# Two mixers of a two-block transformer on one core: x taken ahead of the high parts in a written-out first mixer, the second mixer's first projections in the first one's block, and output products in the second mixer's last head

## The chip, the cores and the metric

The kernel runs on one core of a Trainium2 chip. The metric is the device time of one execution in microseconds (us). A measured time is the median of several runs; the trace comes from one further, profiled execution.

## The reference, cut to what matters

Four layers over 1024 tokens of width 1024, all in float32. The change touches only the first of them:

```python
def rglru_hgrn2_layer(u, w_in, w_out, ...):
    proj = jnp.einsum("bsd,de->bse", u, w_in)
    rg_x, rg_g, hg_q, hg_f, hg_i, hg_g = jnp.split(proj, ...)
    h = rglru_mixer(rg_x, conv_w, conv_b, w_a, b_a, w_x, b_x, lam)
    o = hgrn2_mixer(hg_q, hg_f, hg_i, lb)
    o = o * lax.rsqrt(jnp.mean(o * o, axis=-1, keepdims=True) + RMS_EPS) * g_norm
    merged = jnp.concatenate([h * jax.nn.silu(rg_g), o.reshape(...) * jax.nn.silu(hg_g)], axis=-1)
    return merged @ w_out
```

The first mixer (`rglru_mixer`) takes the x branch through a causal convolution of 4 taps, makes two sigmoid gates of it by 64-wide block matrices, forms `a = exp(log_a)` and `b = sqrt(1 - a*a) * (gate_i * xc)`, and runs the linear recurrence `h = a*h + b` over the tokens. The second (`hgrn2_mixer`) is gated linear attention with 8 heads of width 128, in chunks, with a decay per channel. `merged` has 2048 columns and is multiplied by a 2048 x 1024 matrix. An RWKV-7 layer and two hybrid attention layers follow.

## The kernel before

The program is a row of blocks; a block has one instruction stream per engine, and all engines meet at its end before the next begins. TensorE (PE) does the matmuls, ScalarE (ACT) and VectorE (DVE) everything elementwise, GpSimd (POOL) splits the very first weights, SyncE (SP) issues the DMAs.

Each float32 product is done in float16 in three matmuls: a value is split into a high part and a low part (`w_hi`, `w_lo`; `u_hi`, `u_lo`; `m_hi`, `m_lo`), and high x high, high x low, low x high are summed in PSUM. A projection (`channel_major`, L131; `token_major`, L147) is 8 blocks of the inner dimension x 2 halves x 3 = 48 matmuls of 128x512, or 192 of 128x128. Weights come in units of 512 KB through a ring of 4 slots: SP loads `stage` (`load_unit`), ACT makes the high part (`split_high`, L109), DVE the low part (`split_low`, L115). `K.w_full[slot]` counts units split, `K.w_free[slot]` units used; SP may load a slot when its unit before has been split, ACT may split when PE has used it. Sources are taken one round ahead.

**First mixer** (`rglru`). Four rounds in a hardware loop (`Fori`), each for two tiles of 128 channels. PE's order in a round: x of tile 0, gate branch of tile 0, x of tile 1, gates of tile 0, gate branch of tile 1, gates of tile 1. The x branch uses PSUM banks 0 and 1, the gate branch 2 and 3. Before an x projection PE waits for `x_taken`, which DVE raises (L476) once ACT has copied the x before to `xb` (L425); the first is raised at the end of DVE's setup (L467), a softplus of `lam`. DVE does the convolution (L477 to L482), the product of the gate branch (L486), then the low parts of the next weights. After both tiles ACT does tanh, exp, square and square root, DVE the scan, and its product goes to `m_hi` (ACT, L450) and `m_lo` (DVE, L508). ACT takes the next round's x at the head of that round, so behind both `m_hi` copies.

**Second mixer** (`hgrn2`). PE projects f, q, g and v of head 0 first. Its start waits for `g_taken`, which DVE raises (L798) behind its setup: memsets, and the lower bounds `lb` and `oml` from a softmax (to L795), for which ACT does one exp (L757). `take_f` on ACT (two sigmoids, L679 and L680) needs f and `raw_free`, also raised there, and comes in ACT's order behind `lb_ready`. g may be projected when f is taken, v when q is. In the steady state a head's five level batches of small float32 matmuls (L603), the transposition of k (L613), the state steps (L621), the output (L629, L630) and the norm (L637) stand between the projections of the next head. The last head has no next one, so only those stand there. Its norm comes after it, alone.

**Output projection** (`project_out`, tag out0). First half (output columns 0 to 511): for each of 8 units of `w_out`, for each of 8 token tiles t, 6 matmuls into bank t (L1063). Units 0 to 3 are in the ring slots at the start, split during head 6. Second half: for each t, all 8 units from a held copy. SP's order is low-rank weights, gain, held units 0 to 3, x (8 loads of 512 KB, L1019), ring units 4 to 7, held units 4 to 7. ACT and DVE split in that order.

## Time and profile before

| | |
|---|---|
| three runs | 3682.11, 3686.03, 3684.61 us; median 3684.61 |
| the profiled execution | 3681.23 us, span 3679.2 us |
| PE busy | 3348.3 us, 91% of the span |
| DVE, ACT, POOL busy | 1877.1, 1406.7, 551.2 us |
| TensorE clock granted, mean | 0.961 of 2.4 GHz |
| start-up, to the first mixer's block | 0 to 46.7 us |
| first mixer | to 293 us |
| second mixer | to 839 us |
| output projection out0 | 840.5 to about 1013 us |

Times within a view are microseconds from the span's start. A row of a timeline is start, duration, engine, line, operation, output and inputs; in brackets stands how long the engine had been idle and who released it. "DVEq" or "PEq" is a semaphore instruction of that engine's queue. A busy PE of 100% does not mean full speed: matmuls overlap, so what counts is the time from the start of one to the start of the next.

### The profile page before, as it was taken

How to read it: one execution, taken by the hardware profiler on the slowest of the kernel's cores; microseconds unless marked ns; L12 is line 12 of the kernel's file. 1: busy time of each engine (PE TensorE's matmuls, PEld its weight loads, DVE VectorE, ACT ScalarE, POOL GpSimd, SP SyncE). 2: the span in 40 equal slices, each digit the busy share in tenths (PEclk: the TensorE clock that was granted, in tenths of full speed). 3: DMA queues.
4: the chain of work that ended last, by engine and by line, in shares of the span. 5: the costliest groups of instructions: out<-in, count | busy, mean ns of one | idle time of the engine just before them, and what ended most of it. 6: DMA issues, size and time to landing. Idle time of an engine off the chain costs nothing. (4 is left out here: it accounts for less than half of the span.)

```text
span 3679.2 us, 72862 instructions
## 1 busy us (share of the span) xinstructions
PE 3348.3 (91%) x32106; PEld 2085.2 (57%) x32106; DVE 1877.1 (51%) x2548; ACT 1406.7 (38%) x2026; POOL 551.2 (15%) x350
## 2 busy tenths in 40 slices
PE   6987999978979898999998899989889999899889
PEld 3334666663434343999996466647434566657334
DVE  4654566662253833666663566644352366633442
ACT  3553444442354632333332445533211355523211
POOL 3000000002000001333331133200150232100330
PEclk9998999979989999999999999999999999999999
DMA  5101110104035643111113111020120211020211
GB/s 166 34 23 50 30 40 29 40 0 149 1 107 118 153 115 114 64 64 64 63 45 105 52 46 40 2 62 24 39 82 27 66 38 35 1 68 18 62 62 46
DMA packets 308329, 215.24 MB, mean 59 GB/s; under 512 B 125411, under 2 KB 283950, under 8 KB 305454
## 3 DMA queue, kind: packets, MB, share of 16 engines
q1 hardware_dynamic: 307608, 210.70, 19.2%
q8 instruction: 230, 3.77, 0.4%
q10 hardware_dynamic: 442, 0.37, 0.0%
q14 instruction: 49, 0.40, 0.0%
HBM read 173.26 MB, written 41.98 MB: 59 GB/s over the span
## 5 line engine op out<-in xcount | busy, mean ns | idle before, releaser
L142 PE MATMUL psum<-u,w_hi 128*128 128x512 f16 x2816 | 855.8, 386 | 103.1 <-DVEq L798 32.0
L142 PE MATMUL psum<-u,w_lo 128*128 128x512 f16 x1408 | 542.4, 385 | 0.0
L142 PEld LDWEIGHTS psum<-u,w_hi 128*128 128x128 f16 x2816 | 279.1, 100 | 452.4 <-issue 55.6
L97 POOL TENSOR_TENSOR w_hi<-stage,w_scale 128x1024 f16<-128x1024 f32 x52 | 99.4, 1912 | 1244.8 <-PE psum L142 600.0
L1063 PE MATMUL psum<-w_hi,merged 128*128 128x512 f16 x768 | 236.1, 389 | 24.9 <-PEq L2887 9.1
L115 DVE SCALAR_TENSOR_TENSOR w_lo<-stage,w_hi 128x1024 f16<-128x1024 f32 x124 | 149.3, 1220 | 186.1 <-ACT w_hi L109 186.0
L2475 DVE CUSTOM_DVE_ANT_0 probs_att<-psum,bias_att 128x1024 f32<-128x1024 f32 x128 | 156.8, 1225 | 167.8 <-PE psum L2287 167.6
L142 PEld LDWEIGHTS psum<-u,w_lo 128*128 128x128 f16 x1408 | 139.8, 99 | 172.8 <-issue 11.9
L2265 PE MATMUL psum<-u,w_hi 128*128 128x512 f16 x768 | 231.6, 383 | 6.3 <-PEq L966 6.3
L1063 PE MATMUL psum<-held_hi_out,merged 128*128 128x512 f16 x768 | 231.0, 379 | 0.0
L157 PE MATMUL psum<-w_hi,u 128*128 128x128 f16 x2048 | 173.2, 219 | 0.0
L157 PE MATMUL psum<-w_lo,u 128*128 128x128 f16 x1024 | 172.3, 219 | 0.0
L142 PE MATMUL psum<-mix_b_rp,w_hi 128*128 128x512 f16 x512 | 153.6, 382 | 11.9 <-DVE mix_b_rp L1569 11.4
L157 PEld LDWEIGHTS psum<-w_hi,u 128*128 128x128 f16 x2048 | 158.0, 98 | 4.9 <-issue 4.6
L2384 ACT ACTIVATE probs_att<-probs_att,neg_max_att 128x1024 f32<-128x1024 f32 x128 | 146.3, 1146 | 19.5 <-DVE neg_max_att L2479 19.4
L2315 PE MATMUL psum<-turned_att,merged 128*128 128x128 f32 x1024 | 139.7, 281 | 15.0 <-ACT sq_att L2398 14.6
L2099 DVE COPY_PREDICATED Tt_rc<-tmask_rc,psum 128x256 f32<-128x256 uint32 x192 | 83.6, 444 | 131.9 <-PE psum L1789 110.9
L1063 PE MATMUL psum<-w_lo,merged 128*128 128x512 f16 x384 | 149.4, 389 | 0.0
L2315 PEld LDWEIGHTS psum<-turned_att,merged 128*128 128x128 f32 x1024 | 132.2, 195 | 27.7 <-issue 17.7
L109 ACT ACTIVATE w_hi<-stage 128x1024 f16<-128x1024 f32 x124 | 127.6, 1048 | 53.2 <-PE psum L1063 42.3
L1063 PEld LDWEIGHTS psum<-w_hi,merged 128*128 128x128 f16 x768 | 76.6, 100 | 124.4 <-issue 38.3
L2265 PE MATMUL psum<-u,w_lo 128*128 128x512 f16 x384 | 146.9, 382 | 0.0
(444 smaller groups left out, 6804.8 us busy)
## 6 DMA issues: line engine op xcount, KB each, us to landing
stage<-w_in SPq DMA_DIRECT2D x72, 512.0 KB, 4.0
X<-rwkv_chunks SPq DMA_DIRECT2D x14, 1792.0 KB, 8.0
stage<-ab_w_in SPq DMA_DIRECT2D x48, 512.0 KB, 4.9
stage<-rw_w_in SPq DMA_DIRECT2D x32, 512.0 KB, 4.7
rwkv_chunks<-work_rp SPq DMA_DIRECT2D x26, 512.0 KB, 6.0
stage<-w_out SPq DMA_DIRECT2D x24, 512.0 KB, 5.5
X<-x SPq DMA_DIRECT2D x16, 512.0 KB, 10.7
stage<-ab_w_out SPq DMA_DIRECT2D x16, 512.0 KB, 6.4
```

The source lines that it names most:

```text
L97: pool.tensor_tensor(K.w_hi[:, slot, :], K.stage[:, slot, :], scale, ALU.mult).then_inc(K.w_half[slot], 1)
L109: act.mul(K.w_hi[:, slot, :], K.stage[:, slot, :], W_SCALE).then_inc(K.w_half[slot], 1)
L115: dve.scalar_tensor_tensor(K.w_lo[:, slot, :], K.stage[:, slot, :], W_SCALE, K.w_hi[:, slot, :], ALU.mult, ALU.subtract).then_inc(K.w_full ...
L142: last = pe.matmul(K.psum[:, bank, :], w[:, k, :], u[:, k, cols], start=(k == 0 and n == 0), stop=(k == KT - 1 and n == 2))
L157: last = pe.matmul(out, u[:, k, toks], w[:, k, :], start=(k == 0 and n == 0), stop=(k == KT - 1 and n == 2))
L1063: last = pe.matmul(bank_of(half, t), m[:, 2 * u + k, toks(t)], w[:, at, w_cols], start=(u == 0 and k == 0 and n == 0), stop=(u == UH - 1 a ...
L2099: dve.copy_predicated(Tt[:, q, g * GJ:g * GJ + GJ], mask, data).then_inc(t_ready, 1)
L2265: last = pe.matmul(K.psum[:, PROJ + half, :], w[:, kt, :], u[:, kt, cols(half)], start=(kt == 0 and n == 0), stop=(kt == KT - 1 and n == 2))
L2315: last = pe.matmul(K.psum[:, O_BANK, (i % 4) * P:(i % 4 + 1) * P], v_tiles[h % 2][:, half * 4 + n, :], turned[:, half, n, :], start=(half ...
L2384: act.activation(probs[:, s % 2, m, :], probs[:, s % 2, m, :], ACT.Exp, bias=neg_max[:, s % 2, m:m + 1], accum_out=sums[:, s % 2, m:m + 1] ...
L2475: dve.tensor_tensor_reduce(probs[:, s % 2, m, :], K.bank_pair(m), bias[:, h % 2, at:at + S], LOGIT_UNSCALE, LOWEST, ALU.add, ALU.max, neg_ ...
```

## The change

Five edits:

1. The loops of the first mixer are Python loops on PE, ACT and DVE, so the four rounds are written out. `x_taken` is gone. PE waits for `xb_ready` (ACT's copy itself) instead, and for nothing before the first two projections; the initial `sem_inc`s are gone.
2. ACT takes tile 0's x of the next round after the square roots, before the two `m_hi` copies.
3. Behind its last gates PE projects f and q of head 0 in the first mixer's block. The second mixer starts with g. DVE raises `raw_free`, `q_free` and `g_taken` first thing in its block.
4. `products_ahead` puts 16 pairs (unit, token tile), units 0 to 3 and tiles 0 to 3, between the steps of the last head, into banks 0 to 3, in groups of 3, 3, 2, 3, 1, 2, 2.
5. `project_out` of this layer skips these 16 pairs. Its helper `products` becomes the function `out_products`.

```diff
@@ -364,8 +364,7 @@
...
         lam_ready, y_ready, sl_ready = sem("lam_ready"), sem("y_ready"), sem("sl_ready")
-        gates_done, x_taken, g_taken, gates_taken = (
-            sem("gates_done"), sem("x_taken"), sem("g_taken"), sem("gates_taken"))
+        gates_done, g_taken, gates_taken = sem("gates_done"), sem("g_taken"), sem("gates_taken")
         xb_ready, sig_ready, conv_ready, a_ready = (
@@ -384,12 +383,13 @@
...
             def _(pe):
-                with pe.Fori(0, ROUNDS) as i:
+                for i in range(ROUNDS):
                     rnd = i + first_round
...
-                        pe.wait_ge((x_taken, g_taken)[which], i * 2 + (tl + 1))
+                        if i + tl:
+                            pe.wait_ge((xb_ready, g_taken)[which], i * 2 + tl)
                         channel_major(pe, K, 2 * tl + which, rnd, K.u_hi, K.u_lo,
@@ -410,6 +410,10 @@
...
                     gates(1)
+                pe.wait_ge(xb_ready, KT)
+                channel_major(pe, K, 0, first_round + ROUNDS, K.u_hi, K.u_lo, (0, 1))
+                pe.wait_ge(g_taken, KT)
+                channel_major(pe, K, 1, first_round + ROUNDS, K.u_hi, K.u_lo, (2, 3))
@@ -417,12 +421,18 @@
...
                 act.wait_ge(sl_ready, 1)
-                with act.Fori(0, ROUNDS) as i:
+                def take_x(i, tl):
+                    unit_done(act, K, 2 * tl, i + first_round)
+                    act.mul(xb[:, tl, 3:], K.bank_pair(0), UNSCALE).then_inc(xb_ready, 1)
+                take_x(0, 0)
+                for i in range(ROUNDS):
                     rnd = i + first_round
                     for tl in range(2):
+                        if tl:
+                            take_x(i, 1)
                         act.wait_ge(tile_done, i * 2 + (tl + 1))
-                        unit_done(act, K, 2 * tl, rnd)
-                        act.mul(xb[:, tl, 3:], K.bank_pair(0), UNSCALE).then_inc(xb_ready, 1)
                         unit_done(act, K, 2 * tl + 1, rnd)
@@ -438,13 +448,15 @@
...
                     for tl in range(2):
-                        act.wait_ge(g_taken, i * 2 + (tl + 2))
+                        act.wait_ge(g_taken, i * 2 + (tl + 1))
                         act.activation(r[:, tl, :], r[:, tl, :], ACT.Exp, scale=nsl[:, bass.ds(i * 2 + tl, 1)])
...
                         act.activation(a2[:, tl, :], th[:, tl, :], ACT.Sqrt).then_inc(root_ready, 1)
+                    if i + 1 < ROUNDS:
+                        take_x(i + 1, 0)
                     for tl in range(2):
@@ -464,16 +476,13 @@
...
                 dve.tensor_scalar(nsl[:, :], sl[:, :], -1.0, None, ALU.mult).then_inc(sl_ready, 1)
-                dve.sem_inc(x_taken, 1)
-                dve.sem_inc(g_taken, 1)
                 dve.wait_ge(gate_in, 64)
-                with dve.Fori(0, ROUNDS) as i:
+                for i in range(ROUNDS):
                     dve.tensor_copy(gate_w[:, 0, :, :], wa[:, bass.ds(i * 2, 2), :])
...
                         dve.wait_ge(xb_ready, i * 2 + (tl + 1))
-                        dve.sem_inc(x_taken, 1)
                         dve.tensor_scalar(xc[:, tl, :], xb[:, tl, 3:], tap(3),
@@ -526,7 +535,7 @@
...
-def hgrn2(nc, K, A, first_round, ahead, spare):
+def hgrn2(nc, K, A, first_round, ahead, spare, next_round):
@@ -638,28 +647,52 @@
...
+                early = [(u, t) for u in range(RING) for t in range(EARLY_TILES)]
+                def products_ahead(n):
+                    for _ in range(n):
+                        u, t = early.pop(0)
+                        if t == 0:
+                            pe.wait_ge(K.w_full[u], next_round + 2)
+                        out_products(pe, K, K.psum[:, t, :], (K.w_hi, K.w_lo), u, u, t, KT)
                 def head(h, previous, following):
...
                         project_f(h + 1)
+                    else:
+                        pe.wait_ge(g_taken, H + 1)
+                        pe.wait_ge(v_ready, H + 1)
+                        products_ahead(3)
                     if previous:
                         norm(h - 1)
+                    if not following:
+                        products_ahead(3)
                     level(h, 0)
+                    if not following:
+                        products_ahead(2)
                     level(h, 1)
...
                         project_q(h + 1)
+                    else:
+                        products_ahead(3)
                     level(h, 2)
...
                     turn_k(h)
+                    if not following:
+                        products_ahead(1)
                     state_steps(h)
...
                         project_v(h + 1)
+                    else:
+                        products_ahead(2)
                     output(h)
-
-                project_f(0)
-                project_q(0)
+                    if not following:
+                        products_ahead(2)
                 project_g(0)
@@ -772,6 +805,9 @@
...
             def _(dve):
+                dve.sem_inc(raw_free, 1)
+                dve.sem_inc(q_free, 1)
+                dve.sem_inc(g_taken, 1)
                 lower = K.par[:, COL["lower"]:COL["lower"] + 3 * H].rearrange("p (r h) -> p r h", r=3)
@@ -793,9 +829,6 @@
...
                 dve.tensor_tensor(lb[:, :], ex[:, 1, :], tot[:, :], ALU.mult).then_inc(lb_ready, 1)
-                dve.sem_inc(raw_free, 1)
-                dve.sem_inc(q_free, 1)
-                dve.sem_inc(g_taken, 1)
                 dve.wait_ge(consts_in, 16)
@@ -941,6 +974,20 @@
...
+EARLY_TILES = 4
+def out_products(pe, K, out, weights, at, u, t, UH):
+    w_hi, w_lo = weights
+    for k in range(2):
+        w_cols = slice(k * HALF, (k + 1) * HALF)
+        for n, (m, w) in enumerate(((K.m_hi, w_hi), (K.m_hi, w_lo), (K.m_lo, w_hi))):
+            last = pe.matmul(out, m[:, 2 * u + k, t * P:(t + 1) * P], w[:, at, w_cols],
+                             start=(u == 0 and k == 0 and n == 0), stop=(u == UH - 1 and k == 1 and n == 2))
+    return last
 def project_units(w_out):
@@ -948,7 +995,7 @@
...
 def project_out(nc, K, A, tag, first_round, k_tiles, w_out, post_gain, ahead, load_x=None, next_gain=None,
-                rstd_out=None, low_rank=None, final_gain=None):
+                rstd_out=None, low_rank=None, final_gain=None, early=False):
@@ -1051,20 +1098,6 @@
...
             def _(pe):
-                def terms(unit):
-                    if unit[0] == "held":
-                        return (K.m_hi, held_hi), (K.m_hi, held_lo), (K.m_lo, held_hi)
-                    return (K.m_hi, K.w_hi), (K.m_hi, K.w_lo), (K.m_lo, K.w_hi)
-
-                def products(half, u, t, unit, at):
-                    for k in range(2):
-                        w_cols = slice(k * HALF, (k + 1) * HALF)
-                        for n, (m, w) in enumerate(terms(unit)):
-                            last = pe.matmul(bank_of(half, t), m[:, 2 * u + k, toks(t)], w[:, at, w_cols],
-                                             start=(u == 0 and k == 0 and n == 0),
-                                             stop=(u == UH - 1 and k == 1 and n == 2))
-                    return last
-
                 def turn(t):
@@ -1077,7 +1110,9 @@
...
                     for t in range(TT):
-                        last = products(0, u, t, ("ring", u), slot)
+                        if early and u < RING and t < EARLY_TILES:
+                            continue
+                        last = out_products(pe, K, bank_of(0, t), (K.w_hi, K.w_lo), slot, u, t, UH)
                         if u == UH - 1 and t < TT - 1:
@@ -1090,7 +1125,7 @@
...
                             pe.wait_ge(K.w_full[slot], rnd + 2)
-                        last = products(1, u, t, ("held", u), u)
+                        last = out_products(pe, K, bank_of(1, t), (held_hi, held_lo), u, u, t, UH)
                     last.then_inc(tile_done, 1)
@@ -3115,10 +3150,10 @@
...
             rnd += KT // 2
-            hgrn2(nc, K, A, rnd, project_units(A["ab_w_out"][0])[:RING], room)
+            hgrn2(nc, K, A, rnd, project_units(A["ab_w_out"][0])[:RING], room, rnd + HG_HEADS)
             rnd += HG_HEADS
             project_out(nc, K, A, "out0", rnd, 2 * KT, A["ab_w_out"][0], A["post_norm"][0],
-                        rwkv_units(A, "r", 0), load_x=A["x"][0], rstd_out=rstd_mid, low_rank=low_rank)
+                        rwkv_units(A, "r", 0), load_x=A["x"][0], rstd_out=rstd_mid, low_rank=low_rank, early=True)
             rnd += 2 * KT // RING
```

## Rows read from the trace of the kernel before

A stretch is given in us from the start of the span; "..." stands where lines are left out.

**Rows 1.** Page, part 1: busy us (share of the span) and instructions.

```profile
PE 3348.3 (91%) x32106; PEld 2085.2 (57%) x32106; DVE 1877.1 (51%) x2548; ACT 1406.7 (38%) x2026; POOL 551.2 (15%) x350
```

**Rows 2.** Waits of PE, 50 to 345 us: us in total, times, longest us.

```profile
PE psum L142 <- DVEq L476: 14.5, 3, 4.8
```

**Rows 3.** Timeline, 30 to 54 us: start us, duration us, engine, line.

```profile
43.29 2.12 POOL L101 TENSOR_TENSOR w_lo<-stage,w_hi 128x1024 f16<-128x1024 f32 x1
...
46.78 0.91 DVE L455 MEMSET wa_rg<- 128x1024 f32 x1 [3.10 <-PEq L164]
...
53.91 0.60 PE L142 MATMUL psum<-u,w_hi 128*128 128x512 f16 x1 [12.54 <-DVEq L467]
```

**Rows 4.** Windows: us, busy of PE, PEld, DVE, ACT, POOL; granted clock, DMA.

```profile
86.90:104.10 17.20, 17.20 (x65) 7.60 (x64) 6.81 (x6) 7.09 (x7) 0.00 (x0) 1.00 0.00 0
104.14:124.85 20.71, 20.71 (x97) 9.28 (x95) 14.17 (x11) 13.20 (x12) 0.00 (x0) 1.00 0.17 51
129.85:141.90 12.05, 12.05 (x49) 5.38 (x50) 8.07 (x7) 4.11 (x4) 0.00 (x0) 0.87 0.24 68
...
780.00:811.00 31.00, 16.77 (x69) 14.47 (x68) 26.73 (x33) 15.97 (x17) 0.00 (x0) 0.58 0.00 1
...
925.90:1009.00 83.10, 83.10 (x387) 37.59 (x384) 19.43 (x19) 25.25 (x65) 0.00 (x0) 1.00 0.00 0
```

**Rows 5.** Timelines of ACT and then DVE in the first mixer's rounds.

```profile
104.44 1.11 ACT L432 ACTIVATE X<-psum,par 128x1024 f32<-128x1024 f32 x1 [0.62 <-PE psum L402]
...
127.42 1.28 ACT L425 ACT_TABLE_LOAD   x1
128.72 1.02 ACT L425 ACTIVATE xb_rg<-psum 128x1024 f32<-128x1024 f32 x1
...
268.62 1.11 ACT L432 ACTIVATE X<-psum,par 128x1024 f32<-128x1024 f32 x1 [0.62 <-PE psum L402]
...
127.55 1.23 DVE L508 SCALAR_TENSOR_TENSOR merged<-X,merged 128x1024 f32 x1 [0.23 <-ACT merged L450]
...
133.94 1.28 DVE L482 SCALAR_TENSOR_TENSOR X<-xb_rg,par,X 128x1024 f32<-128x1024 f32 x1 [0.17 <-issue]
```

**Rows 6.** Timelines of DVE, PE and ACT at the second mixer's opening.

```profile
291.74 1.22 DVE L508 SCALAR_TENSOR_TENSOR merged<-X,merged 128x1024 f32 x1 [0.23 <-ACT merged L450]
...
300.29 0.16 DVE L795 TENSOR_TENSOR lb_hg<-ex_hg,tot_hg 128x8 f32<-128x8 f32 x1
...
300.53 1.03 PE L142 MATMUL psum<-u,w_hi 128*128 128x512 f16 x2 [32.05 <-DVEq L798]
...
312.63 1.28 ACT L679 ACT_TABLE_LOAD   x1 [13.21 <-PE psum L142]
...
344.03 1.02 ACT L694 ACTIVATE X<-psum 128x1024 f32<-128x1024 f32 x1 [9.70 <-PE psum L157]
```

**Rows 7.** Timelines of PE and then DVE in the second mixer's last head.

```profile
790.91 10.50 PE L603 MATMUL psum<-qe_hg,ke_hg 128*128 128x64 f32 x48 [4.69 <-DVE qe_hg L837]
...
811.42 3.78 PE L603 MATMUL psum<-qe_hg,ke_hg 128*128 128x128 f32 x16 [4.14 <-DVE qe_hg L842]
...
822.41 0.79 PE L629 MATMUL psum<-st_hg,v_hg 128*128 128x128 f32 x2 [2.94 <-DVE states_hg L922]
...
829.89 1.98 PE L637 MATMUL psum<-states_hg,ones 128*128 128x512 f32 x4 [2.03 <-ACT states_hg L754]
...
794.74 0.72 DVE L851 COPY_PREDICATED st_hg<-room,psum 128x512 f32<-128x512 uint32 x1 [0.69 <-PE psum L603]
```

**Rows 8.** Timelines of PE, ACT, DVE, SP at the output projection's start.

```profile
840.49 0.59 PE L1063 MATMUL psum<-w_hi,merged 128*128 128x512 f16 x1 [8.61 <-PEq L537]
...
865.23 1.06 ACT L109 ACTIVATE w_hi<-stage 128x1024 f16<-128x1024 f32 x1 [10.55 <-DMA stage<-ab_w_out]
...
866.32 2.57 DVE L115 SCALAR_TENSOR_TENSOR w_lo<-stage,w_hi 128x1024 f16<-128x1024 f32 x2 [4.03 <-ACT w_hi L109]
...
853.58 34.17 SPq L71 DMA_DIRECT2D stage<-ab_w_out  x8
```

## The prediction

> **What bounds the kernel now.** I read the page first. TensorE (PE) is busy 91% of the span [rows 1]; no other engine comes near, so time can go only where PE idles, or idles at its lower clock. Then PE's waits in the first mixer: besides the wait at its start and the one at the second mixer's opening, it waits three times, 14.5 us in all, for one semaphore increment on VectorE (DVE), line 476 [rows 2]. The timelines give the moments of each wait [rows 3, 5, 6], the windows price a projection and show the clock [rows 4]. Last I read the last head and the start of the output projection [rows 7, 8], the places where work is moved from and to.
>
> Prices [rows 4]: two projections (96 matmuls) take 20.71 us, so one takes 10.36 and a 128x512 matmul 0.216. 384 products take 83.1 us, again 0.216, so one tile of one unit (6 matmuls) takes 1.30. Gates, projection, gates take 17.2, so one tile's gates take 3.43. A projection begun after an idle stretch takes 12.05 at a granted clock of 0.87: 1.7 us are lost at the 1.2 GHz level.
>
> **Part 1, the first mixer's start.** The first matmul starts at 53.91, after DVE's softplus chain. In the change nothing holds it but the split weights, complete at 43.29 + 2.12 = 45.4, and the block's entry, where DVE starts at 46.78 [rows 3]. So PE starts at 46.8 and everything behind it moves by 7.1 us. ScalarE (ACT) still waits for the softplus (done at 53.9), but its first x is finished at about 59, so the wait hides. What can be late next is the first gates at 79.8, whose gate matrices DVE copied by 61; there are 13 us of slack after the convolution. Bounds: 5 to 7.3 us. I take 7.1.
>
> **Part 2, the three later rounds.** From round to round ACT's first gate sigmoid of tile 1 moves 268.62 - 104.44 = 164.2 in three rounds, 54.7 each [rows 5]. PE's work in a round is 4 x 10.36 + 2 x 3.43 = 48.3. The difference, 6.4, is the 4.8 wait plus 1.7 for the cold restart, less rounding. The wait is for ACT's copy of x, which runs at 128.72 after a table load and after both high-part copies [rows 5]. Taken before them, right after the square roots (about 117, when PE has already finished that x at 114.5), it comes 11 us earlier and PE runs on at 124.9. What is late next is the convolution: PE reaches the gates at 104.14 + 3 x 10.36 = 135.2. DVE ends its low parts at 127.55 + 1.23 = 128.8 whatever ACT does, copies the gate weights, and needs 5.2 us of convolution; in the trace that ended at 133.94 + 1.28 = 135.2, begun at once when x came at 129.7 [rows 5]. Now x is there, so it begins 0.6 to 0.7 earlier and ends near 134.6: hidden, with only 0.6 us of slack. The gate branch's sigmoid follows at about 129.7 and DVE's product at about 136, before the next projection at 138.7. Saved: 3 x 6.4 = 19.3. If the convolution is late by 1.5 per round it is 14.8, and if all that is won is 1 per round, 3. The price of the table load that the loop made ACT repeat (1.28) is off the path. The loops written out cost PE nothing that a row shows: the 384 products of the output projection are written out already and run at 0.216 each.
>
> **Part 3, the second mixer's opening.** Two projections (20.7 us) go in behind the last gates, 268.3 to 289.0, beside DVE's tail, which ends at 291.74 + 1.22 = 293.0 [rows 6]; the cover is 4 us longer than they are, and without it they would cost what hangs over. Before, PE started at 300.53, when the lower bounds were ready (300.29 + 0.16), and the four projections ended at 344.0. Now the third one waits for ACT's two sigmoids of f, which wait for the same lower bounds: 300.5 + table load 1.28 + 0.92 + 1.02 = 303.8. From there 12.05 (cold) + 10.7 (the V projection: 43.5 less 12.05 and 2 x 10.36) = 326.6. Saved 17.4; what follows (splits, the first head) hangs on V's end as before. The other DMAs of that opening stay where they are; a load that lands late would stop ACT's split ahead of its q sigmoid, which has 10 us of slack before V. Bounds: 14 to 17.6.
>
> **Part 4, the last head.** 16 tiles, 96 matmuls, 20.7 us, go into a stretch of 60 us in which PE is half idle. Queued behind each group on PE are the head's own matmuls, so each group is set against its gap. Three tiles (3.9 us) end at 783.9, where the norm starts (783.6 before); three more end at 789.8, before level 0 at 790.9; the two and three that follow fill 792.8 to 801.2, while DVE takes level 1 only at 801.05 and needs levels 2 and 3 at 807 and 811.5. The one between transposition and state steps may cost 0.2. The two before and the two after the output end before or within 0.4 us of what PE then waits for. Against that stands the clock: 0.58 here [rows 4]. With the gaps filled, level 0 ends earlier (DVE waited 0.69 for it), and the output steps, 5.3 us from 822.4 and partly at the low level, take the 3.6 of the head before. The levels at 811.42 stay cold, because no product stands before them [rows 7]. Sum: -0.65 + 0.2 - 1.7 + 0.4, a gain of 1.7. Bounds: 3 gained to 2 lost.
>
> **Part 5, the output projection.** It needs 20.7 us less, if weights come in time. The first four units keep four tiles each: 96 matmuls, 20.7 + 2.2 for the cold start, from 840.5 to 863.4. The fifth unit's weights, though, land at 865.2, behind the 4 MB of x on the same queue; they were issued at 853.58. ACT splits them, and DVE's low part is done at 866.32 + 1.35 = 867.7 [rows 8]. All that hangs on the block's start, not on PE. So PE waits 4.3 us. Units six to eight are there by 872. Then 32 tiles x 1.30 = 41.4, and 1.7 more if the clock falls in the gap: gaps of 4.8 and 4.14 us were both followed by low-level matmuls [rows 4, 7], so I take it. The first half ends at 910.8 instead of 925.9: 15.1 saved. Bounds: 20.7 if the wait did not exist, 13 if two more weights are late.
>
> The Trainium skill, "TensorE: Matmul & The Clock Gate", section "What's actually happening", has the throttled clock as the default that activity releases. The rows agree in so far as each idle stretch above is followed by matmuls at the 1.2 GHz level; by that rule alone, with every gap filled enough, the last head would bring up to 4 us instead of 1.7, and the sum would be 63.
>
> **Sum.** 7.1 + 19.3 + 17.4 + 1.7 + 15.1 = 60.6 us. The profiled execution took 3681.2 (span 3679.2); it becomes 3620.6. The runs' median, 3684.6, is 3.4 above it: 3624.
>
> **Rivals.**
> - The convolution becomes the bound of the rounds. For: 0.6 us of slack. Against: it started 0.3 us after x and should start sooner. If it, or DVE's chain behind it, is late by 3 us a round, part 2 gives 10.3: 3633.
> - The opening or the start does not follow PE: a DMA lands late (the DMA engines are busy to about 67 us). Either takes some 7 us away: 3631.
> - No wait for the fifth unit, or no cold restart after it: up to 5.6 us more, 3618. Against: the DMA order hangs on nothing the change touches.
> - Slower than before: written-out code starves the engines. The place is the first mixer, where 4 x 208 matmuls, once a loop of 208, now stream past, and 192 more follow in parts 3 and 4. The price is a longer issue of each; it decides from 60.6 / 1024 = 59 ns per matmul, 0.216 to 0.275. If each took 80 ns more: 3684.6 - 60.6 + 82 = 3706. Against: 384 written-out products at 0.216 and 100% busy, even while weights load. The Trainium skill, "Runtime: NRT & Kernel Launch", section "Instruction fetch mechanics", says that fetching runs ahead in order and that taken branches are what stalls it; by it the written-out form is the safer one. No run here has the two forms side by side.
> - The change does not do what it says (a wait left that holds PE all the same, such as the one for the gate branch): parts 1 to 3 at half, 3646.
>
> **How the numbers follow.** Main case 0.72; convolution 0.09; late DMA 0.08; no wait 0.05; half the effect 0.04; starved 0.02. The predicted time is the main case's, 3624. The bounds added up give 3616 to 3640; with the smaller rivals inside, I set 3615 to 3638. A measurement of this kernel tells about 0.2%, 7.4 us, from no change: faster 0.96, same 0.02, slower 0.02.
>
> **What would show it.** PE's first 128x512 matmul near 46.8; the period of the rounds 48.3 with PE without gaps until the last gates; the gates waiting for the convolution would show the first rival. Two projections before the second mixer's setup, and the third starting 3.3 us after the lower bounds. In the last head products in the gaps, its length 60.7 less 1.7, and the output steps at 3.6. In the output projection one wait of about 4 us before unit five, and 70 us instead of 85.4 for the first half. A period above 50, a first half above 75, or any stretch of PE at more than 0.23 us per matmul with a clock of 1.00 would prove me wrong.

## The result and the profile after

The changed kernel takes 3622.66 us (median of 4 runs, 3620.94 to 3624.56); the kernel before, in the same session, 3683.36 (3680.57 to 3686.03). The ratio is 0.9836 (95% interval 0.9821 to 0.9852): 60.7 us saved, against 60.6 forecast. The profiled execution took 3623.91, with a span of 3621.8. The same kernel ran again later (e0_again): 3621.05. The agreement to 0.1 us is luck, since the ratio's interval alone is some 5.5 us to either side; what was forecast well are the terms, which the stages below show. One execution of e1_x_late, its profiled one, took 8899.44 us, with each projection at 28.6 us instead of 10.4 and a granted clock of 1.00; what did it is open, and no ratio here counts it.

The page's first part, to be set against [rows 1]: busy microseconds and share of the span. The span is 57.4 shorter. PE is busy 12.0 us less with the same 32106 matmuls; the rest of the gain is time in which it stood idle.

```profile
PE 3336.3 (92%) x32106; PEld 2077.5 (57%) x32106; DVE 1879.8 (52%) x2548; ACT 1401.6 (39%) x2022; POOL 551.8 (15%) x350
```

PE's waits from 40 to 345 us (in total, times, longest). The 14.5 us in three waits of [rows 2] have no successor; what is left is the block's entry, the wait for f's second sigmoid (line 713), two waits in the first head (line 612), and one ahead of the first mixer (line 293).

```profile
PE psum L142 <- ACT X L713: 13.1, 1, 13.1
PE psum L142 <- PEq L164: 5.9, 1, 5.9
PE psum L612 <- DVE qe_hg L870: 3.0, 2, 2.4
PE psum L293 <- DVE scaled_st L270: 0.6, 1, 0.6
```

The start, timeline of PE and DVE (start, duration), against [rows 3]. PE now begins 0.25 us before DVE's first memset, where it began 7.13 behind it.

```profile
49.45 1.01 PE L142 MATMUL psum<-u,w_hi 128*128 128x512 f16 x2 [5.87 <-PEq L164]
...
49.70 0.91 DVE L467 MEMSET wa_rg<- 128x1024 f32 x1 [3.79 <-PEq L164]
```

The rounds, against [rows 5]: timelines of ACT, DVE and PE. The first gate sigmoid of tile 1 (line 442) moves from 100.70 to 245.62 in three rounds, 48.31 each. ACT copies x (line 427) at 113.06, ahead of both high parts and with no table load before it. Before, ACT loaded a table ahead of this copy and another ahead of the gate branch's sigmoid behind it; only the second is left. DVE's two low parts follow each other in 2.43, three taps take 4.01, and the convolution is done at 126.03 + 4.01 = 130.04. PE reaches the gates at 131.57 without a gap.

```profile
100.70 1.11 ACT L442 ACTIVATE X<-psum,par 128x1024 f32<-128x1024 f32 x1 [0.46 <-PE psum L402]
...
113.06 1.00 ACT L427 ACTIVATE xb_rg<-psum 128x1024 f32<-128x1024 f32 x1
...
123.40 1.28 ACT L437 ACT_TABLE_LOAD   x1
...
245.62 1.11 ACT L442 ACTIVATE X<-psum,par 128x1024 f32<-128x1024 f32 x1 [0.46 <-PE psum L402]
...
122.20 2.43 DVE L517 SCALAR_TENSOR_TENSOR merged<-X,merged 128x1024 f16<-128x1024 f32 x2
...
126.03 4.01 DVE L491 SCALAR_TENSOR_TENSOR X<-xb_rg,par,X 128x1024 f32<-128x1024 f32 x3
...
131.57 3.60 PE L402 MATMUL psum<-X,gate_w_rg 128*128 128x512 f32 x8
```

The opening, against [rows 6]: PE ends the two early projections at 266.3. The lower bounds are ready at 277.16. ACT's table load did not wait for them: it began at 276.14, right behind the exp that feeds them, and the sigmoid began when it ended. So g starts 3.3 behind the exp and 2.3 behind the bounds.

```profile
265.92 0.38 PE L142 MATMUL psum<-u,w_lo 128*128 128x512 f16 x1
...
279.42 1.04 PE L142 MATMUL psum<-u,w_hi 128*128 128x512 f16 x2 [13.13 <-ACT X L713]
...
277.00 0.16 DVE L831 TENSOR_TENSOR lb_hg<-ex_hg,tot_hg 128x8 f32<-128x8 f32 x1
...
275.89 0.22 ACT L790 ACTIVATE ex_hg<-ex_hg 128x24 f32<-128x24 f32 x1 [4.07 <-DVE ex_hg L821]
276.14 1.28 ACT L712 ACT_TABLE_LOAD   x1
277.43 1.02 ACT L712 ACTIVATE X<-psum 128x1024 f32<-128x1024 f32 x1
...
302.82 1.02 ACT L727 ACTIVATE X<-psum 128x1024 f32<-128x1024 f32 x1 [9.70 <-PE psum L157]
```

The last head, PE alone, against [rows 7]: products (line 986) in the gaps, level 4 (at 766.91) still cold (at the 1.2 GHz level) behind 5.8 us of idleness, the output steps at full rate (0.39 each), the norm's matmuls at once behind the last products.

```profile
757.22 3.88 PE L612 MATMUL psum<-qe_hg,ke_hg 128*128 128x64 f32 x32
766.91 3.79 PE L612 MATMUL psum<-qe_hg,ke_hg 128*128 128x128 f32 x16 [5.82 <-DVE qe_hg L875]
...
778.27 0.49 PE L638 MATMUL psum<-st_hg,v_hg 128*128 128x128 f32 x2 [0.34 <-DVE states_hg L955]
778.60 0.39 PE L639 MATMUL psum<-qe_hg,states_hg 128*128 128x128 f32 x2
...
784.54 1.88 PE L646 MATMUL psum<-states_hg,ones 128*128 128x512 f32 x4
```

The output projection, against [rows 8], timelines of PE, ACT, DVE, SP. The fifth unit's weights are taken by ACT at 819.98, their low part is done at 822.3, and PE waits 4.44 us.

```profile
795.03 0.58 PE L986 MATMUL psum<-w_hi,merged 128*128 128x512 f16 x1 [8.61 <-PEq L546]
...
822.35 0.39 PE L986 MATMUL psum<-w_hi,merged 128*128 128x512 f16 x1 [4.44 <-DVE w_lo L115]
...
819.98 1.06 ACT L109 ACTIVATE w_hi<-stage 128x1024 f16<-128x1024 f32 x1 [10.50 <-DMA stage<-ab_w_out]
...
821.07 2.57 DVE L115 SCALAR_TENSOR_TENSOR w_lo<-stage,w_hi 128x1024 f16<-128x1024 f32 x2 [5.61 <-ACT w_hi L109]
...
806.75 19.86 SPq L71 DMA_DIRECT2D stage<-ab_w_out  x8
```

Windows of its first and second half, columns as in [rows 4]: 69.97 us for the first, and 83.10 for the second as before.

```profile
795.03:865.00 69.97, 65.53 (x286) 28.82 (x287) 24.44 (x19) 18.06 (x25) 19.44 (x8) 0.95 0.58 195
865.00:948.10 83.10, 83.10 (x387) 37.65 (x385) 19.52 (x20) 25.32 (x65) 0.00 (x0) 1.00 0.00 1
```

Marks taken from the timelines cut each span into stages: PE's first 128x512 matmul; the gates of rounds 0 to 3; ACT's take of V; V of the last head; the output block's start (ACT's table load, some 1 us from PE's start); and ACT's first take of its second half. So the stage called its first half holds one token tile of the second half too, some 11 us.

| us | before | after | e0_again |
|---|---|---|---|
| to PE's start | 53.91 | 49.45 | 46.31 |
| to round 0's gates | 50.53 | 51.25 | 50.31 |
| three periods | 164.18 | 144.92 | 144.93 |
| last gates to V | 75.41 | 57.20 | 56.74 |
| seven heads | 432.38 | 429.86 | 429.58 |
| last V to output block | 64.04 | 62.31 | 62.21 |
| its first half | 96.33 | 81.06 | 80.86 |
| the rest, unchanged | 2742.42 | 2745.75 | 2749.27 |

### The profile page after: what moved, and what is told of

Read it like the earlier page. It is cut to its first block and busy times, and to the rows that moved or that the text cites. A ratio compares the mean times of both kernels' runs of the same rounds, so it can differ in the third digit from the quotient of the medians.

```text
span 3621.8 us, 72693 instructions
## 1 busy us (share of the span) xinstructions
PE 3336.3 (92%) x32106; PEld 2077.5 (57%) x32106; DVE 1879.8 (52%) x2548; ACT 1401.6 (39%) x2022; POOL 551.8 (15%) x350
## 5 line engine op out<-in xcount | busy, mean ns | idle before, releaser
L986 PE MATMUL psum<-held_lo_out,merged 128*128 128x512 f16 x384 | 145.5, 379 | 0.0
```

Of the source, the lines that this page charges most:

```text
L986: last = pe.matmul(out, m[:, 2 * u + k, t * P:(t + 1) * P], w[:, at, w_cols], start=(u == 0 and k == 0 and n == 0), stop=(u == UH - 1 and ...
```

## The experiments

All are compared by medians with the kernel before beside them (3682.64 to 3685.79). A ratio's interval is 0.0013 to 0.002 either way, some 5 to 7 us, so single terms are read from the stages and the medians confirm the large ones.

**e0_again**: the changed kernel once more, measured beside e1, e2 and e3; the other runs are from two later sessions, with 3682.64 and 3685.18 for the kernel before in place of 3685.79.

> The changed kernel unchanged, to have its time beside the others on the same chip and a second profiled execution of it. Theory: 3623 +/- 3; the first mixer's block begins near 46.8 as before (then the 49.5 of the first profile was that execution's), or near 49.5 again (then something in the change moves it). The heads of the second mixer take 61.2 us each but for one or two that take 1.3 to 3.4 more at a lower granted clock, and not the same ones as in the first profile.

3621.05 us (5 runs), ratio 0.9824 (0.981 to 0.9837). The stages are in the table above: all those that the change touches agree within 0.5 us but for the start and round 0. The start is moved by the entry of the block: DVE's first memset starts at 46.78 in the profile of before, 49.70 in that of after, 46.55 here, and between 46.2 and 49.7 over 13 profiles of this case, with nothing in the kernels that goes with it: 49.70 and 46.55 are the same kernel.

**e1_x_late**: x is taken where the old loop took it, behind the high parts; everything stays written out.

```diff
-                        if tl:
-                            take_x(i, 1)
+                        if i or tl:
+                            take_x(i, tl)
...
-                    if i + 1 < ROUNDS:
-                        take_x(i + 1, 0)
```

> The changed kernel, with x of tile 0 of the next round taken behind both high-part copies again, as before. All else stays (written-out loops, no first wait, projections in the first block, products in the last head). Theory: PE waits about 4 us in each of rounds 2 to 4 and restarts cold, so the period of the rounds goes from 48.3 back to about 54, and the time rises by 17 to 19 us, to about 3641. Rival (the written-out code, not the order, made the rounds faster): the period stays within 1 us of 48.3 and the time near 3623. I also look at DVE's drains: if these stay short in this run, they belong to the written-out form.

3635.96 us, ratio 0.9866 (0.9851 to 0.9882): 14.9 more than e0_again, or 14.5 by the median without the long execution, and less than expected. Its stages come from another profile:

**e1_second_profile**: the same kernel.

> The kernel with x taken late once more, for a profile at PE's ordinary speed (the first one was taken in an execution in which every projection took 28.6 us). Theory: rounds of 53 to 54 us, PE waiting about 4 us for ACT's copy of x in each of three rounds, and the projection behind each wait 1.2 to 1.7 us longer; the drains of DVE's convolution short as in the changed kernel, since the code is written out. Five timed runs gave 14.9 us over the changed kernel, so the period should be 48.3 + 5.0 = 53.3.

3632.27 us, one run. PE's waits from 40 to 345 us:

```profile
PE psum L142 <- ACT xb_rg L427: 8.8, 3, 3.0
```

and the timelines of ACT, for the first x taken late, and of PE behind each of the three waits:

```profile
118.88 1.00 ACT L427 ACTIVATE xb_rg<-psum 128x1024 f32<-128x1024 f32 x1
...
119.94 0.60 PE L142 MATMUL psum<-u,w_hi 128*128 128x512 f16 x2 [2.95 <-ACT xb_rg L427]
...
171.37 0.60 PE L142 MATMUL psum<-u,w_hi 128*128 128x512 f16 x2 [2.95 <-ACT xb_rg L427]
...
172.73 1.06 PE L142 MATMUL psum<-u,w_hi 128*128 128x512 f16 x2
...
224.48 1.03 PE L142 MATMUL psum<-u,w_hi 128*128 128x512 f16 x2 [2.95 <-ACT xb_rg L427]
```

The periods are 51.43, 53.11 and 52.76, neither 54.7 nor 48.3. With x late but written out, PE waits 2.95 and not 4.8. On ACT the table load in front of x is gone: the copy of x begins 0.97 behind the start of the second high-part copy, where it began 2.41 behind it (126.31 to 128.72 in before), which makes 1.4 of the difference. The second high-part copy itself begins 0.3 sooner behind the gate sigmoid. DVE's loop head has hardly a part in it: PE began 0.11 behind the end of the copy of x in before and begins 0.06 behind it here. The remaining 0.2 to 1.9 of each period is the lower clock, which came after two of three equal waits. DVE's three taps take 4.01 here as well (121.62 to 125.63), so their missing gaps belong to the written-out form.

**e6_loops**: x ahead, and the rounds as hardware loops again (one round before or behind the loop on PE and ACT).

```diff
-                for i in range(ROUNDS):
+                def round_of(i, first):
...
+                round_of(0, True)
+                with pe.Fori(0, ROUNDS - 1) as i:
+                    round_of(i + 1, False)
...
+                take_x(0, 0)
+                with act.Fori(0, ROUNDS - 1) as i:
+                    round_of(i, True)
+                round_of(ROUNDS - 1, False)
...
-                for i in range(ROUNDS):
+                with dve.Fori(0, ROUNDS) as i:
```

> The changed kernel with hardware loops in the first mixer again: DVE over all four rounds, ACT over the first three and PE over the last three; the order of all instructions, x ahead included, stays. Theory (order, not form, makes the gain; the written-out form costs nothing): period 48.3 to 48.8, time 3623 to 3625. DVE's drains show 0.17 us of idle time each again and the loop head about 0.5, so the convolution of tile 0 ends about 0.9 us later, which is more than its slack of 0.6: the period may rise by 0.3 to 0.5. Rival (written-out code slows issue): the looped one is faster by more than 2 us. Rival (the written-out form is what removed the stall): 3637 or more.

3620.1 us, ratio 0.983 (0.9817 to 0.9844), beside e0_again's 3621.05: no difference. Periods 48.30, 48.31, 48.21. So the order of x alone gives all of part 2, the written-out form alone about 2.3 us a round (54.73 less the mean of e1's periods, 52.43), and the two don't add: with x ahead nothing is left to save. DVE's timeline in this run, and PE's first gate matmul, show the slack that the looped form leaves:

```profile
122.90 0.29 DVE L488 COPY gate_w_rg<-wa_rg 128x256 f32 x1 [0.51 <-issue]
...
125.77 1.28 DVE L498 SCALAR_TENSOR_TENSOR X<-xb_rg,par,X 128x1024 f32<-128x1024 f32 x1 [0.18 <-issue]
127.22 1.28 DVE L498 SCALAR_TENSOR_TENSOR X<-xb_rg,par,X 128x1024 f32<-128x1024 f32 x1 [0.16 <-issue]
...
128.82 0.59 PE L402 MATMUL psum<-X,gate_w_rg 128*128 128x512 f32 x1
```

The convolution is done at 128.50, 0.3 us before the gates; written out it had 1.5.

**e4_old_start**: PE waits for DVE's softplus chain again.

```diff
             def _(pe):
+                pe.wait_ge(sl_ready, 1)
                 for i in range(ROUNDS):
```

> The changed kernel, with PE waiting for the end of DVE's softplus before its first projection, as before. Theory: PE's first 128x512 matmul starts 7.1 us behind the block's entry again and everything moves, +7: about 3628. Rival (the load of the gate matrices or of the weights holds the first round anyway): +3 or less.

3630.78 us, ratio 0.9853 (0.9838 to 0.9868), 9.7 more than e0_again. PE starts at 55.09, 7.23 behind DVE's memset at 47.86. Nothing later takes it back.

**e3_old_opening**: the two projections back in the second mixer's block, and the semaphores that let them start back behind the lower bounds.

```diff
-                pe.wait_ge(xb_ready, KT)
-                channel_major(pe, K, 0, first_round + ROUNDS, K.u_hi, K.u_lo, (0, 1))
-                pe.wait_ge(g_taken, KT)
-                channel_major(pe, K, 1, first_round + ROUNDS, K.u_hi, K.u_lo, (2, 3))
...
+                project_f(0)
+                project_q(0)
                 project_g(0)
...
-                dve.sem_inc(raw_free, 1)
-                dve.sem_inc(q_free, 1)
-                dve.sem_inc(g_taken, 1)
```

(The three increments stand behind `lb_ready` in this kernel.)

> The changed kernel with f and q of head 0 projected in the second mixer's block again, behind the three increments at the end of DVE's setup. Theory: the stretch from the last gates to V's end goes from 57.2 back to 75.4 us, the time to about 3641 (+18). Rival (the first mixer's tail hid them only in part): less than 12 us.

3640.32 us, ratio 0.9877 (0.986 to 0.9893), 19.3 more than e0_again. From the last gates to V it takes 76.29 us against 56.74.

**e5_proj_in_second**: the projections back in the second block, as in e3, but the increments stay early.

```diff
-                pe.wait_ge(xb_ready, KT)
-                channel_major(pe, K, 0, first_round + ROUNDS, K.u_hi, K.u_lo, (0, 1))
-                pe.wait_ge(g_taken, KT)
-                channel_major(pe, K, 1, first_round + ROUNDS, K.u_hi, K.u_lo, (2, 3))
...
+                project_f(0)
+                project_q(0)
                 project_g(0)
```

> The changed kernel with f and q of head 0 back in the second mixer's block, but with the three increments first thing in DVE's stream, as in the change. Theory (the opening is bound by the lower bounds and ACT's two sigmoids when f and q are done before): here f starts at the block's entry, f and q take 22.4 us, g waits for them, and the stretch from the last gates to V's end is 24 + 2 + 12 + 3 x 10.4 = some 69 us, against 57 and 75.4: the time is about 12 us over the changed kernel's, 3633. Rival (what counts is only when the increments come): below 60 us, +3.

3634.85 us, ratio 0.9867 (0.9852 to 0.9882). Gates to V takes 69.92: 12.7 more than after, 6.4 less than e3. So with the projections in the second block the earlier release is worth 6.4, and moving them to the first block is worth the other 12.7. What the early release adds once they are in the first block, no run shows. It can hardly be much: the old release stood right behind the bounds, ready at 277.16, and ACT's first sigmoid begins at 277.43 anyway.

**e2_no_products**: no output products in the last head; the output block does them all.

```diff
-                    for _ in range(n):
+                    for _ in range(0):
                         u, t = early.pop(0)
...
-                        rwkv_units(A, "r", 0), load_x=A["x"][0], rstd_out=rstd_mid, low_rank=low_rank, early=True)
+                        rwkv_units(A, "r", 0), load_x=A["x"][0], rstd_out=rstd_mid, low_rank=low_rank)
```

> The changed kernel without the 16 products in the last head; the output projection does all 384 in its block again. Theory: the output projection's first half goes back to 85.4 us (+15.1) and the last head to 64.0 (+1.7): about 3639.5. If the last head alone costs or gains nothing, 3638. Rival (the products only moved the wait for weights, or the head hid no 20 us): less than 8 us are lost.

3636.15 us, ratio 0.9868 (0.9849 to 0.9888), 15.1 more than e0_again. The stages: last head 63.8 against 62.2, first half 96.3 against 80.9, together 17.0.

**e7_weights_before_x**: SP issues the last four units' weights ahead of x.

```diff
+                ahead_of_x = UH - RING if early else 0
+                for unit in sequence[RING:RING + ahead_of_x]:
+                    load_unit(sp, K, *place[unit], units[unit[1] + (UH if unit[0] == "held" else 0)])
                 if load_x is not None:
...
-                for unit in sequence[RING:]:
+                for unit in sequence[RING + ahead_of_x:]:
```

> The changed kernel with SP loading ring units 4 to 7 of the first output projection ahead of the 4 MB of x. Theory (PE's wait of 4.4 us for the fifth unit's low part comes from x on the queue ahead of it): the wait goes, and with it the restart at the lower clock (1.6), so the stretch from the block's start to the first tile of the second half goes from 81.1 to about 75; time -6, 3616. x then lands about 12 us later, which nobody waits for. Rival (DVE's low parts, slowed beside GpSimd's split of the low-rank weights, hold the fifth unit): the wait stays above 2 us.

3616.84 us, ratio 0.9818 (0.9805 to 0.9832), beside e6's 3620.1, which the runs can't tell apart. The stage shows it: the first half takes 75.67 against 81.06. Waits of PE from 785 to 870 us:

```profile
PE psum L986 <- PEq L546: 8.6, 1, 8.6
PE psum L986 <- DVE w_lo L115: 0.7, 1, 0.7
```

and DVE's low parts with GpSimd's last two instructions in the timelines:

```profile
812.81 8.25 DVE L115 SCALAR_TENSOR_TENSOR w_lo<-stage,w_hi 128x1024 f16<-128x1024 f32 x4
...
811.95 2.69 POOL L1098 TENSOR_TENSOR u<-u,w_scale 128x1024 f32<-128x1024 f32 x1
814.78 2.93 POOL L1100 TENSOR_TENSOR room<-u,room 128x1024 f16<-128x1024 f32 x1
```

The wait of 4.44 is 0.7: it was the place behind x on SP's queue, as predicted. What is late next is DVE. Taken by themselves its four low parts last 2.91, 3.15, 1.21 and 1.21: the first two run beside GpSimd, which works until 817.7, the others behind its end. The first begins at 812.8 and ends at 815.7, the second at 818.8, each 1.1 behind the end of a GpSimd instruction (814.64, 817.71). The Trainium skill, "SBUF — State Buffer", section "SBUF: two separate sides", has a VectorE operation with two SBUF inputs and a GpSimd operation that reads SBUF take turns by an exclusive lock. These rows agree with it; no run here takes GpSimd's work away.

**e8_bounds_first**: DVE's memsets stand behind the lower bounds in the second block.

```diff
-                dve.memset(reset[:, :], 1.0)
-                dve.memset(st[:, :, :], 0.0)
-                dve.memset(ke[:, :, :], 0.0)
...
-                dve.memset(in_chunks(reset[:, :])[:, :, 0:1], 0.0)
...
+                dve.memset(reset[:, :], 1.0)
+                dve.memset(st[:, :, :], 0.0)
+                dve.memset(ke[:, :, :], 0.0)
+                dve.drain()
+                dve.memset(in_chunks(reset[:, :])[:, :, 0:1], 0.0)
```

> The changed kernel with the second mixer's three memsets on DVE (3.6 us with their gaps) behind the lower bounds instead of ahead of them. Theory (the opening is bound by the lower bounds and the two sigmoids, once f and q are done): g starts about 4 us earlier, the stretch from the last gates to V's end goes from 57.1 to 53.1, the time -4, 3618. Rival (g then waits for something else: weights in the ring, DVE's memsets ahead of the q product that V needs): less than 2 us.

3622.1 us, ratio 0.9822 (0.9809 to 0.9836). Gates to V takes 53.51 against 57.20 (e0_again 56.74), so 3.2 to 3.7 in its place; the median doesn't show it.

**e9_fill_level4**: the last head's products are dealt out otherwise: one instead of three behind level 1, four ahead of level 4.

```diff
                     else:
-                        products_ahead(3)
+                        products_ahead(1)
...
+                    else:
+                        products_ahead(4)
                     level(h, 4)
                     turn_k(h)
-                    if not following:
-                        products_ahead(1)
...
-                        products_ahead(2)
+                        products_ahead(1)
```

> The changed kernel with the 16 products of the last head in groups of 3, 3, 2, 1, 4 (ahead of level 4), 2, 1, so that PE's idle 5.8 us ahead of level 4 are filled. Theory (the idle stretch is what sends level 4 to the lower clock): level 4's 16 matmuls take 1.9 us instead of 3.8, DVE takes it 0.8 earlier, the last head (V's end to the block's end) goes from 62.3 to 61.2; time -1, within its uncertainty. Rival (small float32 matmuls run at the low level whatever stands before them): 3.8 us stay.

3626.8 us, ratio 0.9837 (0.9824 to 0.9851). Level 4, which took 3.79 cold, now takes 1.95, so it was the idle time ahead of it that made it slow and not its size. But level 3, before which only one product is left to fill PE's wait, is cold instead, and DVE had finished level 4's input at 763.13, 2.0 us before PE was through with the four products:

```profile
755.37 3.68 PE L612 MATMUL psum<-qe_hg,ke_hg 128*128 128x64 f32 x16 [2.56 <-DVE qe_hg L870]
...
765.17 1.95 PE L612 MATMUL psum<-qe_hg,ke_hg 128*128 128x128 f32 x16
...
761.91 1.22 DVE L875 TENSOR_TENSOR qe_hg<-X,E_hg 128x1024 f32<-128x1024 f32 x1
```

Counted from V, the state steps (line 630) begin 0.5 earlier than in after and the norm 0.9 earlier, the other 0.4 because one product stands ahead of it and not two. The stage is 0.8 shorter (61.53 against 62.31). The median isn't better; whether the 4.7 us over e8 are anything, these runs can't tell.

**e10_all_three**: e7, e8 and e9 together.

> The changed kernel with the three edits together: ring units 4 to 7 loaded ahead of x, the memsets behind the lower bounds, the four products ahead of level 4. Theory: they lie in different stretches and add up, -5.4 -4 -1 = -10: 3611 to 3612, against 3684 of the kernel before a ratio of 0.9805. Rival (they trade with one another, or the next stage takes it back): above 3615.

3612.87 us (5 runs, 3606.37 to 3615.21), ratio 0.9799 (0.9785 to 0.9812): the best version, 72.3 below the kernel before beside it and 8.2 below e0_again's median. Stages: gates to V 52.75, last head 61.58, first half 75.4, together 10.1 less than e0_again.

## Why the prediction was right, step by step

| step | forecast | stages, before to after | by taking it back |
|---|---|---|---|
| 1, start | 7.1 | 7.4, from the block's entry | e4: 7.5 from the entry |
| 2, rounds | 19.3 | 19.3 | e1 and e6: part of it twice over |
| 3, opening | 17.4 | 18.2 | e3: 19.6 |
| 4, last head | 1.7 | 1.7 | e2: 1.6 |
| 5, output projection | 15.1 | 15.3 | e2: 15.4 |
| sum | 60.6 | 61.9 | |

**Part 1** held, and so did its claim that nothing is late next. But "PE starts at 46.8" took the entry of the block for fixed. In this pair the entry came 2.9 later, so PE's start moved by only 4.5.

**Part 2** came out to the tenth, but its slack for the convolution, 0.6 us, was misread. It says that with x there the convolution "begins 0.6 to 0.7 earlier". The copies of the gate weights stand ahead of it on DVE, and in the trace of before they end at 129.79, only 0.23 before it began:

```profile
129.51 0.28 DVE L472 COPY gate_w_rg<-wx_rg 128x256 f32 x1
130.02 0.81 DVE L477 TENSOR_SCALAR X<-xb_rg,par 128x1024 f32<-128x1024 f32 x1 [0.23 <-ACT xb_rg L425]
```

So these rows leave a slack of 0.2 to 0.3, and e6, which keeps the loop, shows 0.3: nearer to the rival than I had it. That the changed kernel has 1.5 comes in the main from gaps that the loop leaves on DVE and that the estimate kept: 0.17 behind each tap, 0.23 between the low parts, 0.5 at the loop's head. That margin was luck. And the table load in front of x is off the path with x ahead, as the prediction says, but in the old order it was part of the wait: written out (e1) it is gone, which is one reason why e1 cost 14.9 and not the 17 to 19 that I expected.

**Part 3** is the term that was mis-sized, by 0.8. The step read "300.5 + table load 1.28 + 0.92 + 1.02". The three durations are right, but they count from the end of ACT's exp (276.11) and not from the bounds (277.16), so g starts 2.3 behind the bounds, not 3.3 (with its rounding the sum had 3.4): 1.1 more gained. Another 0.3 comes from the bounds, which are ready 31.5 us behind the last gates and not 31.8. Against these stands g: from its start to ACT's take it lasts 12.7, at a granted clock of 0.83, where the sum had 12.05 at 0.87, so 0.6 less. In the trace of before the load at 312.63 stood behind PE's projection [rows 6], and so it did in e3 (288.20) and e5 (282.38). But the same trace has a load that runs ahead of the wait, in the first round:

```profile
67.43 1.28 ACT L427 ACT_TABLE_LOAD   x1
76.75 1.02 ACT L427 ACTIVATE a_rg<-psum 128x1024 f32<-128x1024 f32 x1 [8.04 <-PE psum L142]
```

**Part 4** held, and nearly term by term: counted from V, level 4 begins 0.8 earlier (0.65 forecast), the output steps take 1.6 less (1.7), and the norm begins 2.4 behind the output steps instead of 2.0, because of the two products ahead of it (0.4). The 0.2 put down to the product behind the transposition was 0.04 there; level 4 with the transposition takes 0.4 more than before instead. e9 shows that the cold level is worth 1.84 on PE, but not what it costs the stage, since filling the gap made level 4 wait and level 3 cold.

**Part 5** held in both halves. The wait was 4.44 (4.3 forecast), and it hung on SP's order, which e7 shows. The first half took 69.97 against 70.3 from the terms: the idle time was followed by 3.6 us at the low clock level, from 822.80 to 826.40.

The stages sum to 1.3 more than forecast, the medians to 0.1 more. The rest of the program, which the change does not touch, is 3.3 longer in the profile of after, and in the other profiles between 2738.4 and 2752.6. Two heads of seven ran long before (64.2 and 62.5 instead of 61.2) and one after (62.5), each at a granted clock under 1.00. In each of the 12 profiles of the changed kernel and its variants exactly one head of the seven is long, by 1.3, and not always the same one. Windows from V to V of single heads (us; busy of PE, PEld, DVE, ACT, POOL; clock; DMA), first of before, one whole head and the two long ones:

```profile
588.46:649.67 61.21, 59.10 (x478) 41.04 (x478) 38.81 (x49) 29.36 (x30) 0.00 (x0) 1.00 0.12 34
649.67:713.87 64.20, 62.44 (x478) 42.48 (x478) 38.92 (x49) 29.46 (x29) 0.00 (x0) 0.95 0.11 33
713.87:776.41 62.54, 60.77 (x478) 41.63 (x478) 38.91 (x49) 29.46 (x29) 0.00 (x0) 0.97 0.08 25
```

and of after, the long one:

```profile
547.75:610.26 62.51, 60.75 (x478) 41.98 (x478) 38.90 (x49) 29.46 (x29) 0.00 (x0) 0.97 0.12 34
```

The same 478 matmuls cost 1.3 to 3.0 us more in the long ones. The profile pair's 57.4 us of span come from 61.9 so: -2.9 for the entry, +2.5 for the heads, -3.3 for the rest, -0.7 in round 0. What makes such a stretch fall where it does, no run here shows.

**The rivals.** The convolution as bound: no, but with the loop kept only 0.3 us stood between (e6), written out 1.5. A late DMA: no. Written-out code starving the engines: e6 sets the forms side by side, 3620.1 looped and 3621.05 written out, with the same period of 48.3; 80 ns a matmul would have been 82 us. No wait for the fifth unit: e7 had to change SP's order to get it. Half the effect: the three waits are gone, and the idle time at the start and at the opening fell from 12.5 and 32.0 to 5.9 and 13.1.

## What to carry to other kernels

When the bounding engine waits for a copy on another engine, look at what stands in that engine's queue ahead of the copy, before making the copy faster: one step moved up was worth the whole 19 us, and the written-out form nothing beside it. Work for the next phase pays twice where it fills a wait that exists anyway. Where the work can't be moved, look at what releases its buffers: with the projections left in the second block, releasing them first thing was worth 6 us of the 19. Effects that remove the same wait do not add, so take each back by itself, and read the result from the stage where it acts, since runs tell no less than 5 us apart.

## What the runs showed of the hardware

- ACT's table load can run ahead of the wait of the instruction that it serves, and then costs nothing: in before it ran at 67.43, and its sigmoid began at 76.75, when PE let it. It does not always: at 312.63 in before, 288.20 in e3 and 282.38 in e5 it came behind PE's projection, and in after (276.14) 0.26 us of it stuck out behind the bounds. What decides, no run here shows.
- In a hardware loop DVE shows 0.16 to 0.18 us of issue between taps that depend on each other (1.28 each); written out, three run in 4.01.
- Three equal idle times of 2.95 us on PE were followed by matmuls at 2.4 GHz throughout, by 1.4 us of them and then the 1.2 GHz level, and by the low level at once (granted clock of the whole projection 1.00, 0.84 and 0.87). The Trainium skill, "TensorE: Matmul & The Clock Gate", section "What's actually happening", calls the number of slow matmuls at the start of a kernel run-variable; these rows show the same within one execution.
- A low part of 128x1024 on DVE took 2.91 and 3.15 us beside GpSimd and 1.21 behind its end (e7).
